# A state-space mixer's scans over four-token steps: one 128-wide matrix within four tokens, powers of the step in B and C

## The reference

```python
p = h @ w_in[l]                      # u, v (512 each), s_in (256), gates (2 x 1024)
br_a = gmlp_spatial_gating(...)
def s5_direction(u, lam_re, lam_im, log_dt, b_re, b_im, c_re, c_im, reverse):
    lam_bar = jnp.exp(lam * dt)
    b_bar = ((lam_bar - 1.0) / lam)[:, :, None] * bmat
    bu = jnp.einsum('gph,blgh->blgp', b_bar, u)
    _, states = lax.associative_scan(_ssm_combine, (a, bu), axis=1, reverse=reverse)
    return jnp.real(jnp.einsum('ghp,blgp->blgh', cmat, states))
y = s5_direction(forward) + s5_direction(reverse) + d_skip * s
y = gelu(y); y = y * sigmoid(y @ w_glu + b_glu)
merged = g_a * (br_a @ w_up_a[l]) + g_b * (br_b @ w_up_b[l])
x = x + merged @ w_out[l]
```

## Time and profile before

| what | us |
|---|---|
| median of 3 runs | 2282.79 (2281.96 to 2285.68) |
| profiled execution | 2288.16 |
| its span in the trace | 2286.7 |
| PE busy, share of the span | 2002.3, 88% |
| DVE busy | 612.3, 27% |
| ACT busy | 305.7, 13% |
| POOL busy | 184.2, 8% |
| mean granted clock of PE, of full speed | 0.917 |

### The profile page before, as it was taken

The page is one execution under the profiler, slowest core; times in us unless marked ns, Lnnn a source line. Parts: engine busy times, 40 slices in busy tenths (PEclk is TensorE's granted clock), DMA queues, the critical chain, the costliest instruction groups (busy, mean ns, idle before and its releaser), DMA issues.

```text
span 2286.7 us, 18966 instructions
## 1 busy us (share of the span) xinstructions
PE 2002.3 (88%) x8169; PEld 802.3 (35%) x8169; DVE 612.3 (27%) x917; ACT 305.7 (13%) x459; POOL 184.2 (8%) x140
## 2 busy tenths in 40 slices
PE   7989999849999958769999669998999898998986
PEld 3434444343333323223344423333333333333332
DVE  3591001140000135998822311111010001111112
ACT  2230000111010023332310210000000000000001
POOL 0000000010000012655510000000000000000000
PEclk9999999959999979879999779999899999999898
DMA  6111142246989851110034369999999999999995
GB/s 224 63 45 65 40 144 103 81 145 252 388 359 375 353 216 37 37 37 0 0 133 189 123 276 428 428 428 427 428 428 427 428 427 428 428 429 427 429 427 214
DMA packets 68248, 589.77 MB, mean 258 GB/s; under 512 B 5440, under 2 KB 6848, under 8 KB 36800
## 3 DMA queue, kind: packets, MB, share of 16 engines
q1 hardware_dynamic: 59616, 556.02, 58.8%
q10 hardware_dynamic: 4448, 17.80, 2.0%
q0 software_dynamic: 4096, 14.68, 1.9%
HBM read 575.91 MB, written 12.58 MB: 257 GB/s over the span
## 4 chain that ended last, share of the span: by engine, by line
PE 46%; DMA 17%; DVE 10%; issue 3%; ACT 3%; POOL 0%; SPq 0%; ACTq 0%; DVEq 0%; POOLq 0%
PE ps L1844 11%; PE ps L1816 10%; PE ps L233 7%; PE ps L819 6%; DMA ring<-in_w_up 6%; DMA ring<-in_exp_w_up 5%; DMA AR<-in_w_up 5%; PE ps L1797 4%; PE ps L242 3%; PE ps L1523 2%; DVE AR L1958 1%; PE ps L257 1%; PE ps L1430 1%; DVE AR L1351 1%; DVE AR L1375 1%
## 5 line engine op out<-in xcount | busy, mean ns | idle before, releaser
L233 PE MATMUL ps<-AR,ring 128*128 128x512 f32 x1128 | 500.2, 605 | 3.4 <-DVE AR L1366 2.3
L233 PEld LDWEIGHTS ps<-AR,ring 128*128 128x128 f32 x1128 | 217.4, 194 | 286.7 <-issue 278.2
L1958 DVE TENSOR_TENSOR AR<-AR,ps 128x512 f32<-128x512 f32 x128 | 82.7, 685 | 787.8 <-PE ps L1797 787.8
L1816 PE MATMUL ps<-ring,AR 128*64 128x512 f32 x1184 | 262.1, 596 | 12.0 <-DMA ring<-in_w_up 8.8
L819 PE MATMUL ps<-ring,AR 128*32 128x512 f32 x1536 | 256.6, 620 | 14.2 <-DMA ring<-in_exp_w_up 10.7
L1816 PE MATMUL ps<-AR 128*64 128x512 f32 x864 | 191.4, 594 | 9.8 <-DMA AR<-in_w_up 6.3
L819 PE MATMUL ps<-AR 128*32 128x512 f32 x768 | 164.2, 593 | 0.0
L1844 PE MATMUL ps<-ring,AR 128*64 128x512 f32 x576 | 148.1, 674 | 7.4 <-issue 6.6
L1816 PEld LDWEIGHTS ps<-ring,AR 128*64 128x64 f32 x1184 | 90.4, 138 | 179.3 <-issue 157.4
L819 PEld LDWEIGHTS ps<-ring,AR 128*32 128x32 f32 x1536 | 73.7, 114 | 141.3 <-issue 139.9
L1797 PE MATMUL ps<-AR 64*128 64x512 f32 x256 | 104.8, 667 | 18.5 <-DVE AR L1958 17.8
(11 more groups left out here) (298 smaller groups left out, 1490.1 us busy)
## 6 DMA issues: line engine op xcount, KB each, us to landing
ring<-in_w_up SPq DMA_DIRECT2D x38, 2048.0 KB, 18.6
ring<-in_w_gate SPq DMA_DIRECT2D x36, 2048.0 KB, 21.5
ring<-in_w_down SPq DMA_DIRECT2D x36, 2048.0 KB, 25.7
AR<-in_w_gate SPq DMA_DIRECT2D x28, 2048.0 KB, 22.2
AR<-in_w_down SPq DMA_DIRECT2D x28, 2048.0 KB, 24.8
AR<-in_w_up SPq DMA_DIRECT2D x26, 2048.0 KB, 20.7
ring<-in_w_in SPq DMA_DIRECT2D x15, 2048.0 KB, 9.1
ring<-in_exp_w_up SPq DMA_DIRECT2D x15, 2048.0 KB, 13.7
```

What stands on the lines that cost most here:

```text
L233: x = PE.matmul(ps, l, r, start=i == 0, stop=i == len(pairs) - 1)
L1816: x = PE.matmul(GU[2 * m + f // 2][64 * (f % 2):64 * (f % 2) + 64, :], XS[n // 2 % 2][:, k * P + 64 * b:k * P + 64 * b + 64], w[:, kk_, f ...
L1958: DV.tensor_tensor(XK[:, o:o + T], XK[:, o:o + T], CO[i % 2][:, :], ALU.add).then_inc(d_co, 1)
```

## The change

It moves the recurrence from one token at a time to four. Tokens are split into 128 places of four (`S4`: 4 tokens x 32 channels of a group pair on 128 partitions, 128 places along the free dimension). The inputs of four tokens are brought into one state by B times powers 0 to 3 of the step (`BS`, transposed into `B4`), the state then advances with the fourth power (`r4`, turns of 4 tau), and the four outputs come from C times powers 1 to 4 (`CQ`). What the four tokens of a place give each other, with the skip term, is one 128x128 matrix per group pair, `TP`, put together from the product `G` of B and the powers of C. The 16 steps become 4 groups g of four pairs; a table, a turn and a product take four pairs of 128 places at once, and the scans are 8 per group, over 128 places. POOL keeps one iota. B's rows and the states lie in ring slot 1, so the slots of the mixer's loads are dealt out anew, `2pa` is loaded in the mixer, and `2glu` and the loads behind it wait for the outputs. The Gelu of branch B reads banks 6 and 7 on ACT in 32 pieces, which put the tokens back in order.

```diff
-        slot += [(2, 3, 0, 1)[i % 4] for i in range(n1 - at["2s"])]
-        slot += [(6, 7, 8, 0, 1, 2, 3)[i % 7] for i in range(len(loads) - n1)]
+        slot += [2, 3, 0, 2, 3, 0, 3, 1, 2, 0, 3, 1, 2, 0]
+        slot += [(6, 7, 8, 3, 1, 2, 0)[i % 7] for i in range(len(loads) - n1)]
...
+        def pe_v(g):
+            h = g % 2
+            PE.wait_ge(k_b4c, 2 * g + 2)
+            for i in range(2):
+                b = pe_bank(("V", g, i))
+                for j in range(4):
+                    x = PE.matmul(b[:, sl(j, P)], B4[:, g, i, j, :], S4[:, sl(4 * h + j, P)], start=True, stop=True)
+                x.then_inc(k_v, 1)
+
+        def pe_tp():
+            PE.wait_ge(k_tp, 1)
+            for j in range(8):
+                PE.matmul(Y5[j // 4][:, sl(j % 4, P)], TP[:, j, :], S4[:, sl(j, P)], start=j % 4 == 0, stop=False,
...
+        def pe_y(g):
+            d, h = divmod(g, 2)
+            PE.wait_ge(k_x, g + 1)
+            for j in range(4):
+                for i in range(2):
+                    c = j * P + 1 - d
+                    x = PE.matmul(Y5[h][:, c:c + 127], CQ[i][:, 4 * g + j, 1 - d:5 - d, :], XS4[:, g, i, j, d:d + 127],
...
+        def dve_powers(A, B, p, re, im, signs):
+            lr, li = (v[p].unsqueeze(2).to_broadcast([P, 16, 32]) for v in (LR, LI))
+            DV.tensor_tensor(X4[0], A, lr, ALU.mult)
+            DV.tensor_tensor(X4[1], B, li, ALU.mult)
+            DV.tensor_tensor(X4[2], B, lr, ALU.mult)
+            DV.tensor_tensor(X4[3], A, li, ALU.mult).then_inc(s_dv, dv())
+            DV.wait_ge(s_dv, dv.n)
+            for d in range(2):
+                r = slice(8 * d, 8 * d + 8)
+                DV.tensor_tensor(re[d], X4[0][:, r, :], X4[1][:, r, :], signs[0])
+                x = DV.tensor_tensor(im[d], X4[2][:, r, :], X4[3][:, r, :], signs[1])
...
+        def dve_scan(g):
...
+            DV.tensor_tensor(W0, co_t, vr, ALU.mult)
+            DV.tensor_tensor(Z0, si_t, vi, ALU.mult)
+            DV.tensor_tensor(W1, co_t, vi, ALU.mult)
+            DV.tensor_tensor(Z1, si_t, vr, ALU.mult).then_inc(k_mm, 1)
+            DV.wait_ge(k_mm, g + 1)
+            DV.tensor_tensor(W0, W0, Z0, ALU.add)
+            DV.tensor_tensor(W1, W1, Z1, ALU.subtract).then_inc(s_dv, dv())
+            DV.wait_ge(s_dv, dv.n)
+            for j in range(4):
+                r = r4[:, 4 * g + j:4 * g + j + 1].to_broadcast([P, P])
+                DV.tensor_tensor_scan(Z0[:, j, :], r, W0[:, j, :], 0.0, ALU.mult, ALU.add)
+                x = DV.tensor_tensor_scan(Z1[:, j, :], r, W1[:, j, :], 0.0, ALU.mult, ALU.add)
...
+            for i, (a, b, o) in enumerate(((co_t, si_t, ALU.subtract), (si_t, co_t, ALU.add))):
+                DV.tensor_tensor(W0, a, Z0, ALU.mult)
+                DV.tensor_tensor(W1, b, Z1, ALU.mult).then_inc(s_dv, dv())
+                DV.wait_ge(s_dv, dv.n)
+                x = DV.tensor_tensor(XS4[:, g, i, :, rv], W0, W1, o)
...
+            for j in range(4):
+                r = slice(32 * j, 32 * j + 32)
+                for q in range(4):
+                    t = TP[32 * q:32 * q + 32, j::4, :]
+                    x = DV.tensor_copy(t[:, :, 32 * q:32 * q + 32], GD[r, :, :])
+                    if q < 3:
+                        x = DV.tensor_copy(t[:, :, 32 * q + 32:P], G[r, :, 0, 32:P - 32 * q])
+                    if q > 0:
+                        x = DV.tensor_copy(t[:, :, 0:32 * q], G[r, :, 1, P - 32 - 32 * q:96])
...
         def sp_mixer2():
-            for n in range(at["2pa"] + 1, n1):
+            for n in range(at["2pa"], n1):
+                if n == at["2glu"]:
+                    SP.wait_ge(k_y, 2)
                 sp_load(n)
```

More of the change, by code:

```diff
@@ L1054, in sp_experts @@
         def sp_experts():
-            for n in range(at["eg3"], at["2pa"] + 1):
+            for n in range(at["eg3"], at["2pa"]):
                 sp_load(n)
@@ L1471, in pe_mixer2 @@
                 x.then_inc(b_sp, 1)
+            b = pe_bank("G")
+            PE.wait_ge(k_cq, 1)
+            for h in range(2):
+                for d in range(2):
+                    for i in range(2):
+                        for j in range(4):
+                            n = 8 * d + 4 * h + j
+                            x = PE.matmul(b[32 * j:32 * j + 32, sl(2 * h + d, P)], BT[i][:, n, :], CQ[i][:, n, d:d + 4, :],
+                                          start=i == 0, stop=i == 1, tile_position=(0, 32 * j), skip_group_check=True)
+            x.then_inc(k_g, 1)
+            PE.wait_ge(k_s4a, 1)
+            PE.wait_ge(k_s4v, 1)
+            pe_v(0)
+            pe_v(1)
             pa, sa, na = weights("2pa", 4)
@@ L1557, in act_mixer2 @@
                 AC.activation(TW[c % 3], tb("ga", c), ACT.Sigmoid, bias=p2("bgate", c, 1)).then_inc(a_ga, 1)
+            for h in range(2):
+                AC.wait_ge(k_y, h + 1)
+                for j in range(4):
+                    for q in range(4):
+                        x = AC.activation(BB[32 * j:32 * j + 32, h * T + q:(h + 1) * T:4], Y5[h][32 * q:32 * q + 32, sl(j, P)],
+                                          ACT.Gelu)
+                x.then_inc(a_y5, 1)
             for j in range(4):
@@ L1590, in dve_mixer2 @@
             DV.wait_ge(s_p2, 16)
-            dve_norm(R3, XT, H2, p2("g12"), TW[1])
+            dve_norm(R3, XT, H2, p2("g12"), MM[3])
             def op(x):
@@ new lines, in dve_mixer2 @@
+            DV.wait_ge(s_5a, A_BT)
+            for i in range(2):
+                for d in range(2):
+                    DV.tensor_copy(BS[i][:, 8 * d:8 * d + 8, 3 - 3 * d, :], BT[i][:, 8 * d:8 * d + 8, :])
+            for p in range(1, 4):
+                re, im = ([BS[i][:, 8 * d:8 * d + 8, (3 - p, p)[d], :] for d in range(2)] for i in range(2))
+                x = dve_powers(BT[0], BT[1], p, re, im, (ALU.subtract, ALU.add))
+                if p < 3:
+                    op(x)
+            x.then_inc(k_bs, 1)
@@ L1650, in dve_mixer2 @@
+            DV.wait_ge(k_bs, 1)
+            DV.wait_ge(b_s, 2)
+            for j in range(4):
+                for q in range(4):
+                    x = DV.tensor_copy(S4[32 * q:32 * q + 32, sl(4 + j, P)], bank[t_bank["s", 1]][32 * j:32 * j + 32, q::4])
+            x.then_inc(k_s4v, 1)
             for a in range(4):
@@ L1664, in dve_mixer2 @@
                 DV.tensor_tensor(v, v, p2("lnb"), ALU.add).then_inc(d_vn, 1)
+            for p in range(1, 5):
+                re, im = ([CQ[i][:, 8 * d:8 * d + 8, (p, 4 - p)[d], :] for d in range(2)] for i in range(2))
+                x = dve_powers(Cr, Ci, p, re, im, (ALU.add, ALU.subtract))
+                if p < 4:
+                    op(x)
+            x.then_inc(k_cq, 1)
+            DV.wait_ge(k_cq, 1)
+            DV.wait_ge(k_tb, 2)
             for m in range(4):
```

383 lines of the change are left out of this document (176 added, 207 removed).

## The result

| | before | after |
|---|---|---|
| median of the runs on one chip, us | 2284.23 (4 runs) | 2184.35 (4 runs) |
| profiled execution / its span | 2288.2 / 2286.7 | 2184.5 / 2183.0 |
| end of the `s` product to the last output matmul | 392.4 | 296.2 |
| of it: PE busy / granted clock / standing still | 354.1 / 0.92 / 38.3 | 291.9 / 0.99 / 4.3 |
| DVE / POOL busy in it | 247.2 / 149.7 | 139.7 / 0.0 |

The ratio is 0.956 (0.9544 to 0.9577): faster, by 99.9 us. The predicted 2199 is 14.6 us too long and its range began at 2185, 0.65 us above the median, so the time lies outside it. Two more sets of runs of the same kernel gave 2186.14 and 2184.27.

A forecast was written before the change was run, and what follows sets the result against it. The mixer, held by DVE's step operations and then PE, was taken to set the kernel's end. PE work of 295.6 us, 1 of later start and 11 of waits and slow clock gave 2199, range 2185 to 2226.

The forecast's parts named there:

- Slow clock: One stretch of slow PE clock in the mixer, priced at 5 us from 6.3 lost behind a wait of 5.5.
- the later start: Eight cold transposes ahead of the mixer's norm make all that follows 1 us later.
- wide matmuls: The mixer's 308 matmuls of 128x512 behind the `s` product, at 0.86 us each at full clock: 264.9 us.
- 1: DVE's powers of B for the transposes behind v; PE waits about 3.5 us for copies of `s`.
- 2: DVE's powers of C for G: ready at 958, PE there at 958.7, so no wait and no cover.
- 3: TP, for the bank of the first ya: PE waits 0 to 4 us, taken as 2.5.
- 4: Scans: DVE needs 11.4 us per group, PE 12.3, so DVE stays ahead by 0.9 us per round.
- the rule on them: DVE copies starting another group of 32 partitions wait for earlier ones, 0.12 us each, 4 in all; sum would be 2201.
- Weights not hidden: Rival, chance 0.12: weight loads of the 72 full-weight matmuls are exposed, costing 40 us instead of 17: 2222.
- DVE falls behind: Rival, chance 0.20: DVE's work up to TP takes longer than figured and PE waits: 2212 to 2235.
- Small products let the clock fall: Rival, chance 0.03: small products between wide groups halve PE's clock from G to the last outputs: 105 us more, 2304.
- The end does not move with the mixer: Rival, chance 0.02: expert weights already stream before 1228 us, the gain is absorbed and time stays at 2283.

The follow-up runs named there:

- the run without waits: Kernel after, with both halves of the copies of `s` and the 24 copies from G's bank into TP on ScalarE: 2176.72 us, beside the kernel after 2178.84.
- after_again: The kernel after run once more, unchanged: 2186.14 us, 98.0 under the kernel before.

## Why the prediction was right or wrong

The direction and the mechanism were right. The sum was not: the step that failed is the sizing of its terms for slow clock, for waits and for PE's small products, G above all. Slow clock was put at 5 us and measured 1.7, G at 5 and measured 1.9, the waits at 6 and measured 4.3, the spatial product at 5 and measured 3.7, the later start at 1 and measured 0. All erred to the same side. The low end of the range, PE alone at 2187 less a little, kept the full prices of PE's terms, and a time below it had a chance of 0.03. Another 2 to 3 us come from a term put at nothing, the early load of `2pa`.

| term of the sum, us | predicted | measured |
|---|---|---|
| start of the main part later | 1.0 | 0 |
| wide matmuls | 264.9 | 265.1 |
| 32 transposes | 3.7 | 3.6 |
| V, TP, outputs (72) | 17 | 16.1 |
| G | 5 | 1.9 |
| spatial product | 5 | 3.7 |
| waits | 3.5 + 2.5 | 2.2 + 2.1 |
| slow clock | 5 | 1.7 |
| main part, from 890.4 or 882.5 | 307.6 | 296.2 |

- **PE's own work**: predicted 295.6, measured 289.7 in the run without waits. Of the 5.9, G is 3.1: I scaled it from a spatial product that had run at 0.59 of the clock and kept the upper half of 3 to 6. The spatial product is the same error, 1.3: its row was slow clock, and I took back only a part of it. V, TP and the outputs are 0.9. At full clock G takes 0.03 us a record and the spatial product 0.06.
- **Slow clock**, the largest single miss: I took the 6.3 us behind a wait of 5.5 as the price of any wait. At 2.2 and 2.1 us of wait the trace shows 0 and 1.7, and in after_again the second shows 0 (14.00 us for the 32 records, with the same wait of 2.10). At 5.4 and 8.3 us, in two pieces, it is 2.5 and 3.0, and at 58.9, in two pieces, 3.4 (the busy POOL). A price read behind one long wait didn't hold for these.
- **The handoffs.** 1: powers of B were due 28.1 us after the `s` product and came after 25.4, so the wait was 2.2 and not 3.5. It is, as predicted, a wait for the copies of `s`, not for the powers. 2: powers of C met the end of the spatial product within 0.1 us (946.9 and 947.0), no wait and no cover, as predicted. 3: 2.1 us of wait, predicted 2.5. 4: no wait in a round.
- **The copies and the rule on them.** The 16 copies of `s`, each to another group of 32 partitions, take 0.30 us from start to start (4.8 us in all), which I had as 4 us. Those into TP show what happens within a few rows: L1750 and L1752 start before the copy ahead of them in the same group of 32 partitions has ended (0.11 and 0.20 us behind its start, which took 0.18 and 0.27), and L1748, the first of the next group, only when it has (0.21 behind a start, 0.20 long).

```profile
953.77 0.18 DVE L1748 COPY AR<-AR 32x64 f32<-32x64 f32 x1
953.88 0.27 DVE L1750 COPY AR<-ps 32x128 f32<-32x128 f32 x1
954.08 0.20 DVE L1752 COPY AR<-ps 32x64 f32<-32x64 f32 x1
954.29 0.19 DVE L1748 COPY AR<-AR 32x64 f32<-32x64 f32 x1
```

  The trace agrees with the Trainium skill (VectorE: DVE Perf Modes, "Two Vector instructions with no wait between them"). The rule held for the copies; the 2 us that it would have added to the sum (2201) lead away from the measured time all the same, since the powers were ready 2.7 us earlier than figured.
- **Weights not hidden** (the first rival) is refuted by the pitch of 0.111 per record and by the 64 extra matmuls. The trace differs from what the Trainium skill (TensorE: Matmul & The Clock Gate, "The mechanism") lists as its finding, that weight loads overlap only between different row groups; a sentence ahead of that list also allows it for a background weight buffer.
- **DVE falls behind** did not happen: its operations cost the uncontended prices. The run with a busy POOL shows that it would have, by 56 us, had POOL worked without a pause. The prediction read two things of POOL wrongly, and the sum rests on neither. Its operations per step were six, not four. And the row taken for an idle POOL, L1376 at 679 ns, was not: POOL worked beside it for 0.5 of its 0.68 us, as these rows of the kernel before show.

```profile
919.38 0.68 DVE L1376 TENSOR_TENSOR AR<-AR 128x512 f32<-128x512 f32 x1
919.98 1.75 DVE L1377 TENSOR_TENSOR AR<-AR 128x512 f32<-128x512 f32 x1
...
919.53 1.64 POOL L1342 TENSOR_TENSOR AR<-AR 128x512 f32<-128x512 f32 x1 [0.63 <-DVE AR L1375]
```

  So beside POOL some operations pay and some don't; 0.68 is the uncontended price even so, as the kernel after shows.
- **Small products let the clock fall** did not happen: none of the eight narrow groups between the rounds has a slow stretch.
- **The end does not move with the mixer** did not happen either: there are 1004.2 us from the last output matmul to the end, 1003.9 before.
- **Where the 96 us came from**: PE's matmuls at full clock 327.6 to 290.4 (37; predicted 34), waits 38.3 to 4.3 (34) and slow clock 26.5 to 1.7 (25), the last two together 59 where I had 51. The 327.6 is an estimate, with the prediction's 59 for the step matmuls, and 26.5 is what it leaves of 354.1. The runs name the cause: POOL's width 30.5, the matmuls alone 6.8, the rest of the steps' work on DVE, POOL and ScalarE some 39, and 19 for the two first steps, the chain and what else the change does, which no run took apart.
- Of the miss of 14.6 us, 11.4 lie in the main part and 3.2 outside it: 2 to 3 likely for the load of `2pa` beside the experts, which I had costed at nothing. The rest stays open.

## What to carry to other kernels

Where one engine is fed by another, take work from the feeding engine first: 38.7 us less of busy TensorE gave 6.8 us, and narrower elementwise work on GpSimd gave 30.5, with VectorE busy 53 us less for the same operations. Price a wait by rows of its own length, and ask what the next handoff gives back: 3.2 us of more wait here cost 1.9, slow clock included. When every unsure term of a sum is rounded up, put the low end of the range at the sum of their low ends, not at "no wait at all" with the rest kept.

## What was not expected of the hardware

- A busy GpSimd held up VectorE even in tiny operations. Beside it (128x512 additions of 1.45 us) the 128x16 products and sums of the powers, 0.16 to 0.17 us alone, took up to 1.25 us, and a 128x512 operation with a single SBUF input 1.48 (0.42 in the kernel after). From DVE's timeline in that run:

```profile
906.72 1.48 DVE L1383 TENSOR_SCALAR AR<-AR 128x512 f32<-128x512 f32 x1
...
925.38 1.25 DVE L1670 TENSOR_TENSOR AR<-AR 128x16 f32<-128x16 f32 x1
...
929.38 0.16 DVE L1670 TENSOR_TENSOR AR<-AR 128x16 f32<-128x16 f32 x1
929.58 1.14 DVE L1671 TENSOR_TENSOR AR<-AR 128x16 f32<-128x16 f32 x1
```

- The same wait of 2.10 us, at the same place of the same kernel, had a stretch at half clock behind it in two profiles (15.70 us for 32 records) and none in a third, after_again (14.00 us; its rows are shown in "What lies ahead of the mixer"). In the third the wait some 50 us ahead of it was shorter, 0.89 us instead of 2.2. Whether that is the reason no run shows.
